# Weight loads beside expert gathers, each issued as rows 0 to 119 and rows 120 to 127

## What is computed

```python
q = (x @ w_q).reshape(B, S, PEER_HEADS, 2, PEER_DK // 2)
s = jnp.einsum('bshcd,cnd->bshcn', q, sub_keys).astype(F32)
sv, si = lax.top_k(s, PEER_TOPK)
...
e_idx = jnp.take_along_axis(cand_i, pos, axis=-1)
gate = jax.nn.softmax(best_s, axis=-1).astype(x.dtype)
...
hid = jax.nn.gelu(jnp.einsum('td,ted->te', xt, u[et]), approximate=False)
return jnp.einsum('te,ted->td', gt * hid, v[et])
```

## Time and profile before

| | |
|---|---|
| median of 3 runs | 1543.88 us (1543.83 to 1544.87) |
| span of the profiled execution | 1542.9 us |
| TensorE busy | 88% |
| VectorE busy | 67% |
| ScalarE busy | 45% |
| GpSimd busy | 32% |
| moved by DMA | 596.01 MB, 386 GB/s over the span |

### The profile page before, as it was taken

One profiled execution on the slowest core, in us unless ns is written; L12 is line 12 of the kernel. 1 busy time (PEld: TensorE's weight loads), 2 busy tenths in 40 slices (PEclk: granted clock), 3 DMA queues, 4 the chain that ended last, 5 costly groups with the idle time before them and its releaser, 6 DMA issues.

```text
span 1542.9 us, 16889 instructions
## 1 busy us (share of the span) xinstructions
PE 1358.6 (88%) x5064; PEld 736.7 (48%) x5064; DVE 1038.3 (67%) x2555; ACT 687.5 (45%) x2022; POOL 495.3 (32%) x524
## 2 busy tenths in 40 slices
PE   9999898987898888899999799998879898888886
PEld 8877554442353443445446555444335444333322
DVE  1127877777867777676654587877786867666655
ACT  1122544545544544335554244654453544444443
POOL 0004334333333333333320243343333333333431
PEclk9999999989999999989999899999999999999999
DMA  9539999999999999999996499999999999999996
GB/s 360 192 136 385 392 419 418 420 422 421 421 422 421 415 422 421 420 392 368 421 377 254 193 420 421 421 416 421 421 421 421 414 415 421 422 414 409 414 421 250
DMA packets 91534, 596.01 MB, mean 386 GB/s; under 512 B 10290, under 2 KB 12978, under 8 KB 25268
## 3 DMA queue, kind: packets, MB, share of 16 engines
q0 software_dynamic: 73728, 536.90, 84.1%
q1 hardware_dynamic: 17716, 58.04, 10.0%
HBM read 593.86 MB, written 1.05 MB: 386 GB/s over the span
## 4 chain that ended last, share of the span: by engine, by line
PE 39%; DMA 25%; DVE 20%; ACT 9%; issue 4%; DVEq 2%; POOL 1%; another core or an unknown queue 0%; ACTq 0%; POOLq 0%
DMA uv<-in_peer_uv_dram,expert 25%; PE y L658 22%; DVE uv L1681 8%; PE spare L556 3%; PE y L514 2%; PE px L365 2%; PE y L390 2%; ACT diag L1252 2%; ACT L1244 2%; ACT wts L1246 1%; DVE key_idx L1529 1%; DVE hit L1521 1%; POOL uv L1091 1%; ACT act_hid L1244 1%; ACT L1208 1%
## 5 line engine op out<-in xcount | busy, mean ns | idle before, releaser
L658 PE MATMUL y<-uv,diag 128*128 128x512 f32 x1872 | 915.3, 625 | 157.4 <-ACT diag L1252 156.6
L1681 DVE CUSTOM_DVE_ANT_0 uv<-px,uv 128x1024 f32<-128x1024 f32 x512 | 617.6, 1220 | 314.7 <-DMA uv<-in_peer_uv_dram,expert 299.5
L1091 POOL DMA_INDIRECT uv<-in_peer_uv_dram,expert x512 | 491.8, 961 | 1005.9 <-PE y L658 766.8
L658 PEld LDWEIGHTS y<-uv,diag 128*128 128x128 f32 x1872 | 339.4, 195 | 593.2 <-issue 302.5
L1244 ACT ACTIVATE act_hid<-hid 128x1 f32<-128x1 f32 x512 | 103.0, 201 | 602.6 <-DVE hid L1681 588.9
L1252 ACT ACTIVATE diag<-ident,wts 128x128 f32<-128x128 f32 x468 | 188.0, 402 | 44.5 <-PE y L658 1.5
L1246 ACT ACTIVATE wts<-act_hid,gate 128x1 f32<-128x1 f32 x512 | 150.8, 295 | 16.6
L1244 ACT ACT_TABLE_LOAD x47 | 60.3, 1283 | 0.8
L1693 DVE SCALAR_TENSOR_TENSOR vsum<-uv,wts,vsum 128x1024 f32<-128x1024 f32 x41 | 52.6, 1284 | 7.9 <-ACT wts L1246 4.4
L1681 DVE DVE_READ_ACCUMULATOR2_ANT hid<- 128x1 f32 x512 | 42.2, 82 | 0.0
L1410 DVE TENSOR_TENSOR probs<-spare,bias 128x320 f32<-128x320 f32 x16 | 7.6, 473 | 45.4 <-PE spare L407 45.4
(11 more groups left out here) (307 smaller groups left out, 1301.4 us busy)
## 6 DMA issues: line engine op xcount, KB each, us to landing
uv<-in_peer_uv_dram,expert POOLq DMA_INDIRECT x512
uv<-in_na_w_dram SPq DMA_DIRECT2D x9, 512.0 KB, 8.7
w_q<-in_peer_w_q_dram SPq DMA_DIRECT2D x8, 512.0 KB
uv<-in_mla_w_out_dram SPq DMA_DIRECT2D x8, 512.0 KB, 7.1
out_rows<-in_na_w_out_dram SPq DMA_DIRECT2D x6, 512.0 KB
out_rows<-in_mla_w_out_dram SPq DMA_DIRECT2D x6, 512.0 KB
bias<-in_na_bias_dram SPq DMA_DIRECT2D x16, 160.0 KB, 7.0
w_vu<-in_na_w_dram SPq DMA_DIRECT2D x4, 512.0 KB, 8.8
```

The costliest lines, as they stand in the source:

```text
L658: last = T.matmul(Y[t][:, c, :], diag[:, acc_no(n) % DIAGS, :], uv[:, n % RING, 1, c * 512:(c + 1) * 512], start=False, stop=(k == TOPK - ...
L1091: pool.indirect_dma_start(uv[:, n % RING, :, :].rearrange("p h d -> p (h d)"), None, uv_table, bass.IndirectOffsetOnAxis(ap=expert[:, g % ...
L1681: V_.tensor_tensor_reduce(out=rows, in0=px[:, :, :], in1=rows, scale=1.0, scalar=0.0, op0=ALU.mult, op1=ALU.add, accum_out=hid[:, k:k + 1] ...
```

## The change

Thirty loads are each issued as two, first rows 0 to 119 and then rows 120 to 127, and the waits for them count twice as much. They are all 13 side loads (one of them, `("Q", 6)`, early in layer 0 before the gathers), the queries of heads 4, 6 and 7 for layer 0 and of heads 4 and 5 for layer 1 (ten tiles), and the seven loads of latent weights: 18176 KB, of which 12544 KB fall among the gathers of layer 0, 4608 KB in those of layer 1 or just ahead of them, and 1024 KB elsewhere. The gathers and all other loads stay as they are.

```diff
+CUT = 120
...
+        cut_kept = [(0, 4), (0, 6), (0, 7), (1, 4), (1, 5)]
+
+        def kept_landed(layer, h):
+            return sum(64 if (l, h) in cut_kept else 32 for l in range(layer + 1))
...
             def side_item(*name):
-                pe.wait_ge(s_side, 16 * (side_no[name] + 1))
+                pe.wait_ge(s_side, 32 * (side_no[name] + 1))
...
-                pe.wait_ge(s_kept[g % PH], 32 * (layer + 1))
+                pe.wait_ge(s_kept[g % PH], kept_landed(layer, g % PH))
...
-                    pe.wait_ge(s_latkv, 16)
+                    pe.wait_ge(s_latkv, 32)
...
+            def cut_load(dst, src, done):
+                sp.dma_start(dst[0:CUT], src[0:CUT]).then_inc(done, 16)
+                sp.dma_start(dst[CUT:P], src[CUT:P]).then_inc(done, 16)
...
-                sp.dma_start(out_rows[:, :], src).then_inc(s_side, 16)
+                cut_load(out_rows[:, :], src, s_side)
...
                 for c in range(2):
-                    sp.dma_start(kept[h][c], peer_w_q[layer, h, c]).then_inc(s_kept[h], 16)
+                    if (layer, h) in cut_kept:
+                        cut_load(kept[h][c], peer_w_q[layer, h, c], s_kept[h])
+                    else:
+                        sp.dma_start(kept[h][c], peer_w_q[layer, h, c]).then_inc(s_kept[h], 16)
...
                         for dst, piece, done in loads[h]:
-                            sp.dma_start(dst, piece).then_inc(done, 16)
+                            cut_load(dst, piece, done)
```

More of the change, by code:

```diff
@@ L585, in latents_q @@
                 if some[0] == 0:
-                    pe.wait_ge(s_latq, 16)
+                    pe.wait_ge(s_latq, 32)
                     bank_free(b)
@@ L610, in up_k @@
             def up_k(t, half, b):
-                pe.wait_ge(s_kn, 16)
+                pe.wait_ge(s_kn, 32)
                 bank_free(b)
@@ L620, in up_v @@
             def up_v(t, half, b):
-                pe.wait_ge(s_vu, 16)
+                pe.wait_ge(s_vu, 32)
                 bank_free(b)
@@ L629, in up_q @@
             def up_q(t, half, b):
-                pe.wait_ge(s_qn, 16)
+                pe.wait_ge(s_qn, 32)
                 bank_free(b)
@@ L639, in up_qpe @@
             def up_qpe(t, half, b):
-                pe.wait_ge(s_qrs, 32)
+                pe.wait_ge(s_qrs, 64)
                 bank_free(b)
```

## The result

The changed kernel takes **1615.63 us** (median of 4 runs, 1615.12 to 1616.99), the kernel before on the same chip 1544.38 us (median of 4, 1543.83 to 1544.92). The ratio is 1.0467, with a 95% interval of 1.0454 to 1.0479: 71 us slower. The profiled execution spans 1615.2 us, where the one before spans 1542.9.

What follows compares the result with a forecast made beforehand. The prediction took the DMA engines' pace among the gathers, with one late engine, as the bound; -3.0 (layer 1) - 1.5 (layer 0) + 0.2 = -4.3 us, from 1542.9 to 1538.6, plus 1.0: 1539.6 us, range 1534.0 to 1549.5.

Steps and rivals of the forecast that it cites:

- What bounds the kernel: Among the gathers the kernel runs at the pace of the DMA engines, 90% busy or more in nearly every slice.
- 15 and 8 engines, 8 rows and 1: Each cut load: 120 rows go as 15 engines times 8 rows, the other eight as 8 engines times 1.
- What the left-out engine gets back: The engine carrying no cut loads is spared 31.8 us in layer 0 and 11.8 us in layer 1.
- the tail at 0.06: At the program's end one engine works alone for about 4.5 us, at DMA share 0.06 to 0.07.
- that rival: Late engine, or one nearly as late, among the first eight: slower after every cut load, 5.5 us, 1549.4 us; chance 0.13.
- The first eight pay 5.5: Eight engines carry one eighth more of the cut loads: 4.0 us in layer 0, 1.5 us in layer 1.
- The added issues at nothing: 30 more DMAs on the SP queue, about 0.33 us each, some 10 us, costed at nothing because SP sleeps between loads.
- The dry spells: Layer 0, 660 to 664 and 704 to 708 us: engines ran out of gathers, 4.3 us; forecast to shrink.
- the slow cut loads: Rival: cut loads run slower because eight rows in a run write ports other engines write too; chance 0.11.
- the bound of 43.6 us: Upper bound on the price of slow cut loads, letting the cut loads take twice their time.
- What speaks for it: Around a whole load the two queues take 94.6% and 6.6%, gathers alone 101.5%: nothing is lost beside a load.
- The sign that was announced: Sign of being wrong: in 20 us around a cut load, an SP queue share well above 6.6%.

Runs made afterwards that it cites:

- the loads at the end: Kernel before plus small loads behind the last gathers' issue: nine of eight rows, or four of 15 or 16; 1546.37, 1547.34, 1546.88 us.
- the column halves: The changed kernel with its thirty loads split by columns, all 128 rows in both DMAs; 1545.83 us against 1543.63 for the kernel before.
- the pair: Kernel before plus 24 eight-row loads in layer 1, same 1664 KB, taking every fourth row or eight neighbouring rows; 1551.36 and 1570.15 us.
- eight neighbours: Kernel before plus 24 loads in layer 1, each of eight neighbouring rows, into rooms nothing uses any more; 1570.15 us, ratio 1.0172.
- the kernel with loads of every fourth row: Kernel before plus 24 eight-row loads in layer 1, each taking every fourth row, into rooms nothing uses any more; 1551.36 us, ratio 1.0050.

## Why the prediction was wrong

It forecast 1539.6 us, in a range of 1534.0 to 1549.5; 1615.63 came. Two steps failed. The sum counts only how many bytes an engine carries and keeps every packet at its old length, so the loss of rate beside a cut load is in it at nothing; it was some 64 us (the 69 that cutting by rows costs, less 5 for bytes). And the forecast gains were to come from an engine that isn't the late one. The first made the size of the loss, the second left no gain to set against it. Step by step:

- **What bounds the kernel:** right. The gathers run at the pace of the DMA engines, and the whole loss shows as idle time before the dot products.
- **15 and 8 engines, 8 rows and 1:** the counts hold. A load sends 15 + 8 = 23 small packets instead of 16; 30 x 7 = 210 more are on the page (91744 against 91534).
- **What the left-out engine gets back:** the step that the gain rested on. It asked only how many bytes an engine carries. The left-out engine does get less, but it isn't the late one: the tail at 0.06 is as long as before, and the loads at the end put the late engine among the first eight. The row held against that rival, tells who may carry instruction packets, not who is late. A forecast of -3.0 for layer 1 and -1.5 for layer 0 rested on that; layer 1 lost 18.4 and layer 0 53.9.
- **The first eight pay 5.5:** mis-sized. It counts bytes; the eight-row DMAs cost about 16 us by the estimate above.
- **The added issues at nothing:** right within 2.2 us, which is what the column halves cost.
- **The dry spells:** one after 700 us has moved to 756 to 760 us, but nothing was won by it.
- **The rival that came true** is the third, the slow cut loads, and it was mis-sized twice. Its chance was 0.11, and its price 11 us. It named the cause that the pair shows, rows that fall on other engines than in a gather; that two engines then write into the same part of the memory stays unproven. Two things went wrong in its price. I took a quarter of the upper bound with no row behind the quarter. And the bound of 43.6 us itself was no bound: it let the cut loads take twice their time, and forgot that whoever is in conflict with a load is slowed as well. The gathers' own packets took 52.7 us more. With half rate for both queues and as many bytes of gathers as of loads it would be 2 x 43.6 = 87.2 us, near the 71 measured. But that is no bound either: with eight neighbours 1664 KB cost 18.8 us more, 11.6 us a megabyte, because few engines carried the loads, slowly, and everything beside them ran at little over half rate meanwhile (246 GB/s from 1180 to 1220 us). What counts is how long such a load is in flight.
- **What speaks for it was read as a side remark:** the row of a 128-row load beside a gather at full rate was evidence for the placement as it was. A row in which nothing is lost beside a load tells nothing of a load of another shape. The rule on the ports in the Trainium skill, "SBUF — State Buffer", section "Door 1: The DMA port swizzle", cited there, spoke against the change. The trace of after agrees in direction (229 GB/s in place of 425); it shows no port.
- **The sign that was announced:** in layer 1, around one load of 512 KB (1080 to 1100 us), the SP queue takes 8.9% instead of the 6.6% of the earlier trace rows, and the gathers' queue moves less:

```profile
DMA packets 1116, 7.57 MB, mean 378 GB/s; under 512 B 129, under 2 KB 129, under 8 KB 257
...
q0 software_dynamic: 964, 7.03, 92.5%
q1 hardware_dynamic: 151, 0.52, 8.9%
```

At full rate 20 us carry 8.42 MB (421 GB/s); 7.57 came, so one load of 512 KB costs 2.0 us here: 4.0 us a megabyte, as in the sum over the layer.

## What to carry to other kernels

Where loads run beside gathers or loads of 128 rows at the full DMA rate, keep all 128 rows in one DMA; a load that must be split is split along its columns (2.2 us for 30 loads here, against 50 to 71 us along the rows). A busy share of the DMA engines says nothing of their rate: read the GB/s beside it, and when a transfer is slowed by a conflict, price both sides of it, for as long as the transfer is in flight. An engine that works alone at the end tells that one is late, not which; before leaving one out, find out by a load that burdens a few engines just before the end.

## What was not expected of the hardware

- The placement is worth nearly a factor of two, for both streams: 423 against 234 GB/s with only the order of rows changed, and 425 against 229 GB/s around a cut load, at a DMA share of about 1 in all four.
- Small loads are enough: 24 DMAs of 64 to 80 KB cost 18.8 us more out of place than in place, though no more than eight engines carried each, and packets of the other engines were slowed too.
- The late engine's lag at the end is the same, about 4 to 4.5 us, whether the kernel takes 1544 or 1616 us, and also after the first eight engines, with the late one among them, got 7.9 us more to do in layer 1 (the kernel with loads of every fourth row, where the late engine is alone again from about 1534 to 1538 us):

```profile
1534.00:1536.00 2.00, 1.52 (x5) 0.45 (x3) 0.81 (x2) 0.90 (x3) 0.00 (x0) 1.00 0.07 29
1536.00:1538.00 2.00, 1.90 (x4) 0.60 (x4) 1.23 (x2) 0.55 (x3) 0.00 (x0) 1.00 0.06 25
```

So the lag isn't the sum of what this engine has more to do. In that kernel the DMA share fell to 0.78 and 0.72 from 1200 to 1210 us, right behind the loads, where the kernel before has 0.99: engines without added bytes ran out of gathers there and lost their lead, as a ring of eight slots would have it (GpSimd issued none between 1194.69 and 1206.14 us, waiting for the numbers of the next experts). Why the lag settles at 4 to 4.5 us no run shows. Whether a lag that is taken away in the middle would be back by the end was not tried: no kernel relieved this engine.
